# The last weight group of a two-layer encoder trunk, taken tile by tile

## The chip, the core and the metric

The kernel runs on one core of one Trainium2 chip. The metric is device time in microseconds (us), the median over runs of the whole program. One core has a matrix engine (TensorE, PE in the profile, with its weight loads as PEld), a vector engine (VectorE, DVE), a scalar engine (ScalarE, ACT), GpSimd (POOL) and SyncE (SP). SP and POOL issue DMA transfers here. The engines run their own instruction streams and wait for each other by semaphores.

## The reference

The program computes a two-layer encoder trunk for one sequence of 256 tokens with 2048 features, in float32. What matters for this change is the end:

```python
def rmsnorm(x, g):
    xf = x.astype(jnp.float32)
    y = xf * lax.rsqrt(jnp.mean(xf * xf, axis=-1, keepdims=True) + EPS)
    return (y * g.astype(jnp.float32)).astype(x.dtype)

def sq_relu_mlp(h, w1, w2):
    a = jax.nn.relu(h @ w1.astype(h.dtype))
    return (a * a) @ w2.astype(h.dtype)

    for layer in range(DEPTH):
...
        x = x + sq_relu_mlp(rmsnorm(x, f_norm[layer]), f_w1[layer], f_w2[layer])
    return rmsnorm(x, final_norm)
```

The hidden width of the MLP is 8192. The last operations are therefore the second MLP product of layer 1, its addition to x, and one more root-mean-square norm over the 2048 features of each token.

## The kernel before

**Layout.** Activations lie transposed: a feature is a partition, so x is 16 tiles of 128 features by 256 tokens, `x[:, t, :]`. All large weights come from one tensor `wts` in chunks of 1 MB (128 partitions by 2048 floats), in exactly the order in which they are used. 92 *groups* of four chunks each use them up; a group makes 512 output features (four tiles) from 2048 input features (16 tiles, `kt`). Groups 60 to 91 are the MLP of layer 1; it takes the hidden width in four quarters, each of four groups of the first product and four of the second. Group 91 is the last one and makes tiles 12 to 15 of x.

**Splitting.** Float32 precision comes from splitting each weight and each activation into a rounded part and a remainder of type fp32r, which PE multiplies faster than float32. ACT copies half a chunk (a *piece*, 128x1024) from `raw` to `whi` (L278), DVE subtracts it from `raw` into `wlo` (L579). `whi` and `wlo` have four slots each; a group is eight pieces, and PE frees a slot by counting up `half_free` after each piece. SP refills `raw` when `lo_ready` says that DVE is through with it (L242).

**A group on PE** (`group`, L1030 and L1032): for each piece, for each of its two `kt`, for each of four output tiles n, one product of `whi` with both parts of the activation (512 columns) into bank 4·par+n, and one of `wlo` with the rounded part (256 columns) onto the upper half of the same bank. So all four tiles of a group end together. `par` alternates between banks 0 to 3 and 4 to 7. The three operands are accumulated in two halves of a bank, which have to be added: ACT copies the upper halves into `cross` (L271, `copy_cross`), DVE adds the lower ones to it into `total` (L597, `leave_psum`), and adds that to x (L855, `onto_residual`).

**The norm.** Behind each group of the last quarter, `norm_part` has ACT square the four new tiles of x into `padded` (L316) and DVE sum them over the tiles (L619) into `ssum` (L625, L622). With the last of the four, PE multiplies `ssum` with a matrix of ones (L1065, `mean_squares`), which gives every partition the sum over all 2048 features; ACT takes the root (L323), DVE the reciprocal (L639, `rms_of`). Meanwhile ACT has multiplied x by the gain of the final norm into `conv`, one instruction per tile (L488). DVE multiplies four tiles at a time by `rms` (L985), and POOL sends each four tiles out, 512 KB, when they are ready (L262). One float32 product on PE, such as L1065, stands in the trace as two MATMUL records.

**Order.** Nothing is planned by a program: each engine's order is written out by hand. ACT and DVE split the weights of the *next* group between the steps of the present one (`split(G, 0)`, `split(G, 1)` and so on; piece k of it is piece k+3 of group G+1), so that during the steps of group 90 the last five pieces of group 91 are split, and nothing is left to split behind that. In the last quarter, PE runs the same loop as for the other ones; the loop body is 8 groups long.

## Time and profile before

| | us |
|---|---|
| median of 3 runs | 2287.17 |
| lowest and highest of these runs | 2283.44, 2287.83 |
| time of the profiled execution | 2285.45 |
| its span in the trace | 2283.5 |
| last record in the chain of waits, start | 2277.69 |
| output transfers, kind of queue and traffic | software_dynamic, 2.10 MB |
| granted clock over the span | 0.989 |

The page gives each engine's busy time as a share of the span; a chain followed back from the last instruction; groups of instructions by line, with the mean of one in ns. A *window* is the same for a stretch of time, and its clock column is the share of full speed (2.4 GHz) that TensorE was granted: 0.50 is the lower of its two levels, 1.2 GHz. DMA transfers have a time *to landing*, from issue to the end of their last packet. Between the last landing and the end of the span nothing stands in the trace.

### The profile page before, as it was taken

To read this page: it belongs to the slowest core of one execution; us is meant where nothing else is said; L and a number is where in the kernel's file an instruction comes from. 1 tells how busy PE (TensorE), PEld (TensorE's weight loads), DVE (VectorE), ACT (ScalarE), POOL (GpSimd) and SP (SyncE) were. 2 spreads that over 40 slices of the span, in tenths; PEclk is the share of its full clock that TensorE was granted. 3 is DMA by queue.
4 is the path that set the end of the run, shared out by engine and by line. 5 is a ranking of instruction groups with operands and counts; after the bars stand their busy time and mean duration, and the time that the engine had idled before them with its cause. 6 is when DMAs were issued, how large, how long until landed. Compare 5 with 4: busy or idle time off the path is not lost.

```text
span 2283.5 us, 36015 instructions
## 1 busy us (share of the span) xinstructions
PE 2198.2 (96%) x14110; PEld 2023.7 (89%) x14110; DVE 1562.1 (68%) x1809; ACT 972.6 (43%) x1042; POOL 11.5 (1%) x25
## 2 busy tenths in 40 slices
PE   7999999889999999999999999899999999999996
PEld 7988898889999999999999888788899999999995
DVE  8676567467765765765674999977665665665765
ACT  4544344344444544544442100155444444444553
POOL 0000000000000000000000000000000000000000
PEclk9999999999999999999999999999999999999998
DMA  6432233255555555555554444244555555555553
GB/s 226 178 112 91 98 123 121 84 193 185 202 204 202 198 193 211 197 198 197 203 201 148 151 158 153 76 163 167 203 199 198 192 206 200 201 202 202 199 192 123
DMA packets 55864, 396.84 MB, mean 174 GB/s; under 512 B 6497, under 2 KB 6881, under 8 KB 8545
## 3 DMA queue, kind: packets, MB, share of 16 engines
q1 hardware_dynamic: 54288, 389.32, 47.0%
q0 software_dynamic: 1488, 6.29, 1.0%
q8 instruction: 63, 1.03, 0.2%
q14 instruction: 25, 0.20, 0.0%
HBM read 393.49 MB, written 2.10 MB: 173 GB/s over the span
## 4 chain that ended last, share of the span: by engine, by line
PE 77%; DVE 14%; issue 4%; ACT 3%; DMA 2%; DVEq 0%; ACTq 0%; SPq 0%; POOL 0%
PE ps L1030 40%; PE ps L1032 20%; DVE work L925 4%; PE ps L1057 4%; DVE wlo L579 3%; PE ps L1005 3%; PE ps L1007 3%; PE ps L1009 3%; PE ps L1116 2%; DMA raw<-in_wts 1%; ACT whi L278 1%; DVE sq_part L619 1%; PE ps L1181 1%; PE ps L1180 1%; DVE work L686 0%
## 5 line engine op out<-in xcount | busy, mean ns | idle before, releaser
L579 DVE TENSOR_TENSOR wlo<-raw,whi 128x1024 fp32r<-128x1024 f32 x672 | 817.3, 1224 | 493.4 <-ACT whi L278 479.6
L278 ACT ACTIVATE whi<-raw 128x1024 fp32r<-128x1024 f32 x672 | 705.9, 1057 | 714.3 <-PE ps L1032 362.2
L1030 PE MATMUL ps<-hid,whi 128*128 128x512 f32 x2304 | 755.7, 382 | 5.8 <-DVE hid L958 3.3
L1030 PE MATMUL ps<-xg,whi 128*128 128x512 f32 x2048 | 672.0, 382 | 7.1 <-ACT sq_part L323 4.6
L1032 PE MATMUL ps<-hid,wlo 128*128 128x256 f32 x2304 | 628.0, 273 | 0.0
L1032 PE MATMUL ps<-xg,wlo 128*128 128x256 f32 x2048 | 558.2, 273 | 0.0
L1030 PEld LDWEIGHTS ps<-hid,whi 128*128 128x128 f32 x2304 | 435.4, 189 | 67.8 <-issue 3.9
L1032 PEld LDWEIGHTS ps<-hid,wlo 128*128 128x128 f32 x2304 | 442.4, 192 | 0.0
L1030 PEld LDWEIGHTS ps<-xg,whi 128*128 128x128 f32 x2048 | 387.1, 189 | 62.2 <-ACT sq_part L323 5.2
L1032 PEld LDWEIGHTS ps<-xg,wlo 128*128 128x128 f32 x2048 | 393.2, 192 | 0.0
L1005 PE MATMUL ps<-xg,whi 128*128 128x256 f32 x768 | 223.3, 291 | 11.1 <-DVE wlo L579 11.1
L1057 PE MATMUL ps<-work,raw 128*128 128x256 f32 x1024 | 221.5, 379 | 0.0
L1057 PEld LDWEIGHTS ps<-work,raw 128*128 128x128 f32 x1024 | 194.5, 190 | 26.4
L1007 PE MATMUL ps<-xg,whi 128*128 128x256 f32 x768 | 214.7, 280 | 0.0
L1009 PE MATMUL ps<-xg,wlo 128*128 128x256 f32 x768 | 214.3, 279 | 0.0
L925 DVE SCALAR_TENSOR_TENSOR work<-work,dwt 128x256 f32<-128x256 f32 (+1 forms) x492 | 195.5, 480 | 1.0 <-DVE work L908 0.9
L597 DVE TENSOR_TENSOR total<-ps,cross 128x1024 f32<-128x1024 f32 x68 | 98.8, 1453 | 100.3 <-ACT cross L271 97.2
L1005 PEld LDWEIGHTS ps<-xg,whi 128*128 128x128 f32 x768 | 150.8, 196 | 13.6 <-issue 12.7
L1007 PEld LDWEIGHTS ps<-xg,whi 128*128 128x128 f32 x768 | 151.0, 197 | 0.0
L1009 PEld LDWEIGHTS ps<-xg,wlo 128*128 128x128 f32 x768 | 150.9, 196 | 0.0
L271 ACT ACTIVATE cross<-ps 128x1024 f32<-128x1024 f32 x64 | 65.5, 1023 | 112.0 <-PE ps L1032 112.0
L505 ACT ACTIVATE total<-total,pt 128x256 f32<-128x256 f32 x16 | 7.3, 500 | 172.5 <-DVE total L902 172.5
(203 smaller groups left out, 1470.5 us busy)
## 6 DMA issues: line engine op xcount, KB each, us to landing
raw<-in_wts SPq DMA_DIRECT2D x368, 1024.0 KB, 4.8
x<-in_xt SPq DMA_DIRECT2D x4, 512.0 KB, 7.8
x<-in_xt POOLq DMA_DIRECT2D x1, 2048.0 KB, 9.7
out_t<-work POOLq DMA_DIRECT2D x4, 512.0 KB, 3.3
work<-in_rows POOLq DMA_DIRECT2D x12, 128.0 KB, 3.8
ct<-in_consts SPq DMA_DIRECT2D x1, 768.0 KB, 6.3
work<-in_w_s POOLq DMA_DIRECT2D x4, 128.0 KB, 4.3
dwt<-in_dw SPq DMA_DIRECT2D x1, 248.0 KB, 5.0
```

The costliest lines, as they stand in the source:

```text
L271: return nc.scalar.activation(dst, src, ACT.Copy)
L278: nc.scalar.activation(whi[:, i % SPLIT].rearrange("p a b -> p (a b)"), raw[:, r, HALF * (i % 2):HALF * (i % 2) + HALF], ACT.Copy).then_in ...
L579: tt(wlo[:, i % SPLIT].rearrange("p a b -> p (a b)"), raw[:, i // 2 % RAW, HALF * (i % 2):HALF * (i % 2) + HALF], whi[:, i % SPLIT].rearra ...
L597: tt(halves(total[:]), in_order(ps[:, 4 * par:4 * par + 4, 0:T]), in_order(cross[:]), ALU.add).then_inc(banks_free, 1)
L925: ins = stt(acc[t], src, w, acc[t], ALU.mult, ALU.add)
L1005: mm(dst, whi[:, r, k, cols], woven(operand[:, kt, 0, :]), start=(kt == 0 and n % 2 == 0), stop=False, skip_group_check=True)
L1007: mm(dst, whi[:, r, k, cols], woven(operand[:, kt, 1, :]), start=False, stop=False, skip_group_check=True)
L1009: ins = mm(dst, wlo[:, r, k, cols], woven(operand[:, kt, 0, :]), start=False, stop=(kt == KT - 1), skip_group_check=True)
L1030: mm(ps[:, 4 * par + n, :], whi[:, r, k, cols], woven_parts(operand[:, kt]), start=(kt == 0), stop=False)
L1032: ins = mm(ps[:, 4 * par + n, T:2 * T], wlo[:, r, k, cols], woven(operand[:, kt, 0, :]), start=False, stop=(kt == KT - 1))
L1057: ins = mm(ps[:, 4 * par + n, 0:T], raw[:, r, CH_N * k + P * n:CH_N * k + P * n + P], xf[:, kt, :], start=(kt == 0), stop=(kt == KT - 1))
L1116: ins = mm(bank(b)[:, h, :], left[:, h, :], right[:, h, :], start=True, stop=True)
```

## The change

Group 91 is done by a new function on PE, `last_group`, and by new tails on ACT and DVE.

- The weights of group 91 are laid out otherwise in `wts` (on the host, ahead of the run): a chunk is now one output tile with all 16 `kt`, instead of four `kt` of all four tiles. The number of bytes, chunks, pieces and splits is the same.
- PE takes tile after tile, two pieces each. Tiles 12 to 14 use the same two products as before, into banks 4 to 6. Tile 15 has three products of 256 columns instead, all into the lower half of bank 7, so that nothing is left to be added.
- ACT copies the upper half of one bank at a time, squares that tile of x once DVE has added it, and multiplies it by the gain. DVE adds and sums tile by tile (256 wide each). The sum of squares of tile 15 is not added by DVE: PE multiplies `padded[:, 3]` with the ones itself, onto the product of `ssum`, in bank 0.
- The last quarter of the layer-1 MLP is no longer part of PE's loop, but is written out behind it.
- The output leaves in five transfers (4, 4, 4, 2 and 2 tiles) that SP issues, no longer in four that POOL issues. DVE's last four tiles are multiplied in two instructions.

```diff
+OUT_TILES = [(0, 4), (4, 8), (8, 12), (12, 14), (14, 16)]
...
@@ sync
+            for n, (a, b) in enumerate(OUT_TILES):
+                sp.wait_ge(out_raw, n + 1)
+                sp.dma_start(out[:, a:b, :], conv[:, a:b, :]).then_inc(out_done, 16)
+            sp.wait_ge(out_done, 16 * len(OUT_TILES))
@@ gpsimd
-            for j in range(4):
-                pool.wait_ge(out_raw, j + 1)
-                pool.dma_start(out[:, CH_K * j:CH_K * j + CH_K, :], conv[:, CH_K * j:CH_K * j + CH_K, :]).then_inc(out_done, 16)
-            pool.wait_ge(out_done, 64)
@@ scalar
-                for j in range(4):
+                for j in range(3 if last_norm else 4):
                     G = base + 8 * q + 4 + j
...
-            root(4)
+            def gained(t):
+                return nc.scalar.activation(conv[:, t, :], x[:, t, :], ACT.Copy, scale=param("final_norm")[:, t:t + 1])
+
+            act.wait_ge(banks_free, G_END + 1)
+            act.wait_ge(ssum_part, 19)
+            for n in range(4):
+                if n < 3:
+                    act.wait_ge(half_free, SPLIT + 8 * (G_END - 1 - UNSPLIT) + 2 * n + 2)
+                    copy(cross[:, n, :], ps[:, 4 + n, T:2 * T]).then_inc(s["last_cross"], 1)
+                act.wait_ge(s["last_x"], n + 1)
+                nc.scalar.activation(padded[:, n, 0:T], x[:, 12 + n, :], ACT.Square).then_inc(s["last_sq"], 1)
+                ins = gained(12 + n)
+            ins.then_inc(s["gained"], 1)
+            root(4, at=0)
@@ vector
+            for n in range(4):
+                w = x[:, 12 + n:13 + n, :]
+                sums = in_order(ps[:, 4 + n:5 + n, 0:T])
+                if n < 3:
+                    dve.wait_ge(s["last_cross"], n + 1)
+                    link(tt(halves(total[:, n:n + 1, :]), sums, in_order(cross[:, n:n + 1, :]), ALU.add))
+                    tt(w, w, total[:, n:n + 1, :], ALU.add).then_inc(s["last_x"], 1)
+                    dve.wait_ge(s["last_sq"], n + 1)
+                    ins = tt(ssum[:], ssum[:], padded[:, n, 0:T], ALU.add)
+                    if n < 2:
+                        link(ins)
+                    else:
+                        ins.then_inc(ssum_ready, 1)
+                else:
+                    dve.wait_ge(half_free, SPLIT + 8 * (G_END - UNSPLIT))
+                    tt(halves(w), halves(w), sums, ALU.add).then_inc(s["last_x"], 1)
             rms_of(4)
-            for j in range(4):
-                dve.wait_ge(s["gained"], j + 1)
-                w = conv[:, 4 * j:4 * j + 4, :]
-                tt(w, w, by_token(rms[:], 4), ALU.mult).then_inc(out_raw, 1)
+            for a, b in OUT_TILES:
+                dve.wait_ge(s["gained"], min(a // 4 + 1, 4))
+                w = conv[:, a:b, :]
+                tt(w, w, by_token(rms[:], b - a), ALU.mult).then_inc(out_raw, 1)
@@ tensor
+            def last_group(G):
+                pe.wait_ge(banks_free, G + 1)
+                for i in range(8):
+                    pe.wait_ge(lo_ready, 8 * (G - UNSPLIT) + i + 1)
+                    n, r = i // 2, i % SPLIT
+                    hi, lo = (w[:, r].rearrange("p a (b c) -> p (a b) c", c=P) for w in (whi, wlo))
+                    for k in range(8):
+                        kt = 8 * (i % 2) + k
+                        first, last = kt == 0, kt == KT - 1
+                        if n < 3:
+                            mm(ps[:, 4 + n, :], hi[:, k, :], woven_parts(hid[:, kt]), start=first, stop=False)
+                            ins = mm(ps[:, 4 + n, T:2 * T], lo[:, k, :], woven(hid[:, kt, 0, :]), start=False, stop=last)
+                        else:
+                            mm(ps[:, 7, 0:T], hi[:, k, :], woven(hid[:, kt, 0, :]), start=first, stop=False)
+                            mm(ps[:, 7, 0:T], hi[:, k, :], woven(hid[:, kt, 1, :]), start=False, stop=False)
+                            ins = mm(ps[:, 7, 0:T], lo[:, k, :], woven(hid[:, kt, 0, :]), start=False, stop=last)
+                    ins.then_inc(half_free, 1)
+                pe.wait_ge(banks_free, G + 2)
+                pe.wait_ge(ssum_ready, 5)
+                mm(ps[:, 0, 0:T], const("ones"), ssum[:], start=True, stop=False)
+                pe.wait_ge(s["last_sq"], 4)
+                mm(ps[:, 0, 0:T], const("ones"), padded[:, 3, 0:T], start=False, stop=True).then_inc(ms_ready, 1)
...
-                with pe.Fori(1, NQ) as q:
+                with pe.Fori(1, NQ - layer) as q:
...
-            mean_squares(4)
+            base = G_MLP1 + 8 * (NQ - 1)
+            with pe.Fori(0, 2) as i:
+                for par in range(2):
+                    group(base + 2 * i + par, par, xg, None, 0, UNSPLIT)
+            for j in range(3):
+                group(base + 4 + j, j % 2, hid, hid_ready, 20 + 4 * (NQ - 1) + 1, UNSPLIT)
+            last_group(G_END - 1)
@@ kernel
+    w = a["f_w2"][1][(NQ - 1) * D:, D - CH_N:]
+    parts[-1][-4:] = w.reshape(KT, P, 4, P).transpose(2, 1, 0, 3).reshape(4, P, CH)
```

On DVE, the program's end before, from the last subtraction of a piece of group 91 to the last product with `rms`:

```order
L579 TENSOR_TENSOR wlo<-raw,whi 128x1024 [waits hi_ready]
L597 TENSOR_TENSOR total<-ps,cross 128x1024 [waits cross_ready]
L855 TENSOR_TENSOR x<-x,total 128x1024 [waits banks_free]
L619 TENSOR_REDUCE sq_part<-padded 128x256 [waits sq_ready,x_new]
L622 TENSOR_TENSOR ssum<-ssum,sq_part 128x256 [waits ssum_part]
L639 RECIPROCAL rms<-sq_part 128x256 [waits root_ready,ssum_ready]
L985 TENSOR_TENSOR work<-work,rms 128x1024 [waits gained,rms_ready]
L985 TENSOR_TENSOR work<-work,rms 128x1024 [waits gained] x3
```

The same place on DVE now (`work` is the memory of `conv`; `ps` is PSUM; three rows for each of the tiles 12 to 14, then the one that adds tile 15):

```order
L593 TENSOR_TENSOR wlo<-raw,whi 128x1024 [waits hi_ready]
L1000 TENSOR_TENSOR total<-ps,cross 128x256 [waits last_cross]
L1001 TENSOR_TENSOR x<-x,total 128x256 [waits dve_step]
L1003 TENSOR_TENSOR ssum<-ssum,padded 128x256 [waits last_sq]
L1000 TENSOR_TENSOR total<-ps,cross 128x256 [waits last_cross,dve_step]
L1001 TENSOR_TENSOR x<-x,total 128x256 [waits dve_step]
L1003 TENSOR_TENSOR ssum<-ssum,padded 128x256 [waits last_sq]
L1000 TENSOR_TENSOR total<-ps,cross 128x256 [waits last_cross,dve_step]
L1001 TENSOR_TENSOR x<-x,total 128x256 [waits dve_step]
L1003 TENSOR_TENSOR ssum<-ssum,padded 128x256 [waits last_sq]
L1010 TENSOR_TENSOR x<-x,ps 128x256 [waits half_free]
L653 RECIPROCAL rms<-sq_part 128x256 [waits root_ready]
```

The reduction over four tiles is gone; nine instructions stand in its and the addition's place ahead of the one that waits for the last product (L1010).

On ACT, the end of the program before, behind the last copies of pieces:

```order
L278 ACTIVATE whi<-raw 128x1024 [waits half_free,raw_in1] x2
L271 ACTIVATE cross<-ps 128x1024 [waits banks_free,half_free]
L316 ACTIVATE padded<-x 128x4x256 [waits ssum_part,x_new]
L488 ACTIVATE work<-x,pt 128x256 x4
L323 ACTIVATE sq_part<-ps,pt 128x256 [waits ms_ready]
```

And the same place on ACT now:

```order
L278 ACTIVATE whi<-raw 128x1024 [waits half_free,raw_in1] x2
L271 ACTIVATE cross<-ps 128x256 [waits half_free,ssum_part,banks_free]
L571 ACTIVATE padded<-x 128x256 [waits last_x]
L562 ACTIVATE work<-x,pt 128x256
L271 ACTIVATE cross<-ps 128x256 [waits half_free]
L571 ACTIVATE padded<-x 128x256 [waits last_x]
L562 ACTIVATE work<-x,pt 128x256
L271 ACTIVATE cross<-ps 128x256 [waits half_free]
L571 ACTIVATE padded<-x 128x256 [waits last_x]
L562 ACTIVATE work<-x,pt 128x256
L571 ACTIVATE padded<-x 128x256 [waits last_x]
L562 ACTIVATE work<-x,pt 128x256
```

The copy of a tile's upper half now stands behind the square and the gain of the tile before, and L323 (the root) follows as before.

## Rows read from the trace of the kernel before

**Rows 1.** Page, part 1: busy time of each engine.

```profile
PE 2198.2 (96%) x14110; PEld 2023.7 (89%) x14110; DVE 1562.1 (68%) x1809; ACT 972.6 (43%) x1042; POOL 11.5 (1%) x25
```

**Rows 2.** Windows; columns: stretch, its length, busy PE, PEld, DVE, ACT, POOL, clock, DMA.

```profile
2263.50:2284.00 20.50, 1.22 (x2) 0.50 (x2) 10.72 (x9) 3.12 (x6) 2.14 (x4) 0.55 0.25 102
```

**Rows 3.** Chain that ended last, from 2262: start, length, what.

```profile
2262.00 1.03 ACT cross L271
2263.06 1.24 DVE total L597
2264.32 1.24 DVE x L855
2265.58 1.06 ACT padded L316
2266.73 1.91 DVE sq_part L619
2268.67 0.43 DVE ssum L622
2269.15 1.24 PE ps L1065 x2
2270.41 0.48 ACT sq_part L323
2270.98 1.76 DVE rms L639
2272.77 1.22 DVE work L985
...
2275.13 2.28 DVE work L985 x2
...
2277.69 0.53 POOL out_t L262
```

**Rows 4.** Groups by form, whole run: drain of four tiles, one-tile copy from PSUM.

```profile
L597 DVE TENSOR_TENSOR total<-ps,cross 128x1024 f32<-128x1024 f32 x68 | 98.8, 1453 | 100.3 <-ACT cross L271 97.2 <-ACT cross L305 2.5 <-DVE rms L639 0.5
L305 ACT ACTIVATE cross<-ps,pt 128x256 f32<-128x256 f32 x16 | 6.2, 471 | 1.5 <-PE ps L1032 1.5
```

**Rows 5.** Timeline of PE, products of an early group, then of the last: start, length.

```profile
199.84 0.28 PE L1005 MATMUL ps<-xg,whi 128*128 128x256 f32 x1
...
202.18 0.28 PE L1005 MATMUL ps<-xg,whi 128*128 128x256 f32 x1
...
2254.92 0.38 PE L1030 MATMUL ps<-hid,whi 128*128 128x512 f32 x1
...
2261.47 0.38 PE L1030 MATMUL ps<-hid,whi 128*128 128x512 f32 x1
```

**Rows 6.** Timeline of DVE and ACT while the last group runs.

```profile
2253.30 2.36 DVE L579 TENSOR_TENSOR wlo<-raw,whi 128x1024 fp32r<-128x1024 f32 x2
...
2246.95 1.69 ACT L488 ACTIVATE work<-x,pt 128x256 f32<-128x256 f32 x4
```

**Rows 7.** Windows as rows 2, straight PE code and behind it; then timeline of PE.

```profile
1612.00:1696.00 84.00, 84.00 (x513) 77.22 (x514) 59.87 (x49) 41.45 (x40) 0.00 (x0) 1.00 0.54 194
2262.00:2266.00 4.00, 0.00 (x0) 0.00 (x0) 2.45 (x2) 1.45 (x2) 0.00 (x0) 0.93 0.00 0
...
1600.54 0.60 PE L1065 MATMUL ps<-ssum,ct 128*128 128x256 f32 x2
```

**Rows 8.** Output transfers: landing; DMA rate in 40 slices of 2270 to 2283.5.

```profile
DMA to landing us min/median/max: 2.9/3.3/3.6
...
GB/s 0 0 0 0 0 0 0 0 0 0 0 0 0 0 0 0 449 413 425 267 388 388 400 376 352 400 413 376 376 400 425 352 12 0 0 0 0 0 0 0
```

**Rows 9.** Page, part 6, landing on SP; then DMA rate, 40 slices of 0.5:12.

```profile
raw<-in_wts SPq DMA_DIRECT2D x368, 1024.0 KB, 4.8
pt<-in_params SPq DMA_DIRECT2D x1, 97.5 KB, 2.1
...
GB/s 0 0 0 0 52 228 310 299 399 228 256 413 342 413 399 456 427 370 342 399 427 342 399 413 456 485 442 456 456 370 456 427 399 399 342 413 413 442 413 427
```

More of the change, by code:

```diff
@@ L159, in build @@
             "glu_scaled", "gate", "taps0", "taps1", "pivot_sum", "pivot", "acc_init", "first_ln_d", "ln_sq", "ln_stats",
-            "ln_var", "ln_root", "ln_norm", "ln_act", "gained")}
+            "ln_var", "ln_root", "ln_norm", "ln_act", "gained", "last_cross", "last_x", "last_sq")}
         block = ctx.enter_context(nc.Block())
@@ L319, in norm_part, with root @@
                     copy(xg[:, 4 * j:4 * j + 4, 0, :], total[:]).then_inc(xg_hi, 1)
-            def root(n):
+            def root(n, at=7):
                 act.wait_ge(ms_ready, n + 1)
-                nc.scalar.activation(sq_part[:], ps[:, 7, 0:T], ACT.Sqrt, scale=1.0 / D, bias=eps).then_inc(root_ready, 1)
+                nc.scalar.activation(sq_part[:], ps[:, at, 0:T], ACT.Sqrt, scale=1.0 / D, bias=eps).then_inc(root_ready, 1)
             eps, eps_q = param("eps"), param("eps_q")
@@ L882, in mlp @@
                     split(G, 3, 4, 5, 6, 7, skipped=skipped)
-                for j in range(4):
+                for j in range(3 if last and layer else 4):
                     G = base + 8 * q + 4 + j
@@ L980, in _ @@
             mlp(G_MLP1, 1, NQ - 1, True, None)
+            for n in range(4):
[14 more added lines that the diff above has]
+                    tt(halves(w), halves(w), sums, ALU.add).then_inc(s["last_x"], 1)
             rms_of(4)
-            for j in range(4):
-                dve.wait_ge(s["gained"], j + 1)
-                w = conv[:, 4 * j:4 * j + 4, :]
-                tt(w, w, by_token(rms[:], 4), ALU.mult).then_inc(out_raw, 1)
+            for a, b in OUT_TILES:
+                dve.wait_ge(s["gained"], min(a // 4 + 1, 4))
+                w = conv[:, a:b, :]
+                tt(w, w, by_token(rms[:], b - a), ALU.mult).then_inc(out_raw, 1)
         @block.tensor
```

## The prediction

> **What bounds the kernel now.** I start with the busy shares. PE is busy for 96% of the span and no other engine for more than 68% [rows 1]; up to its last product the kernel is as fast as PE gets through its matmuls. This change takes no matmul away, so no gain can come from there, and the next view is the window in which PE is not busy. From 2263.5 to the end, 20.5 us, PE works for 1.22 us [rows 2]. The tail behind the last product is thus a chain of single steps, and the chain of waits gives it in order [rows 3]: the last product ends at 2262.0 (ACT starts at 2262.00), then ACT copy, DVE add, DVE add to x, ACT square, DVE reduction, DVE sum, PE product, ACT root (begins at 2270.41), DVE reciprocal, and from 2272.77 the four multiplications with rms, 1.14 us apart (2.28 for two). The last transfer is issued at 2277.69. From 2262.0 to 2283.5 that is 21.5 us: 8.41 us until the root begins, 2.36 from there to the first multiplication, and 10.7 for multiplying and sending. The reader is to see that nearly every step of the first stretch handles four tiles (1024 wide), although each is independent of the other tiles, and that PE stands idle meanwhile.
>
> **Part 1: the products of group 91.** Tiles 12 to 14 have the same products in another order. A pair (512 and 256 columns) is issued every (2261.47 - 2254.92) / 20 = 0.3275 us, 20 pairs lying between the two rows shown [rows 5]. Tile 15 has 48 products of 256 columns in place of 16 pairs. In the early groups, which use that form, 21 products lie between the two rows shown, (202.18 - 199.84) / 21 = 0.1114 us each [rows 5]. So tile 15 takes 48 x 0.1114 = 5.35 us, not 16 x 0.3275 = 5.24: +0.11. Those early products also go into one bank three at a time, which is the nearest row for what is new in tiles 12 to 14, several products in a row into the same bank. The weights' pieces come in the same number and order, and DVE has the last one ready at 2253.30 + 2.36 = 2255.66 [rows 6], while PE needs it at about 2262.1 - 2.7 = 2259.4. The last quarter's products are now straight code: from 1612 to 1696 PE runs such code and is busy for 84.00 of 84.00 us [rows 7]. I cost it at nothing; fetching instructions is hidden by the products before.
>
> **Part 2: does the tile chain keep up?** DVE is free at 2255.66, when tiles 12 and 13 (ends of their products: 2262.0 less 15.7 and 10.5 us) are done and tile 14 (2256.8) nearly is, so DVE and ACT set the pace, not PE. No row shows these 256-wide forms, except DVE's sum over SBUF, 0.43 us [rows 3], and ACT's copy from PSUM, 0.47 [rows 4]. Reading PSUM while PE writes there costs DVE 1.453 us for four tiles (mean of 68), and 1.24 where PE is idle [rows 4, 3]; I take 0.43 x 1.453 / 1.24 = 0.50 for L1000. ACT instructions in a row follow every 1.69 / 4 = 0.42 us [rows 6]. Each handoff costs about 0.04 (from 2262.00 + 1.03 to 2263.06, for instance) [rows 3]. One round: DVE add 0.54, DVE onto x 0.46, ACT square 0.51, ACT gain 0.42, ACT copy of the next tile 0.42, sum 2.35 us. DVE's order is strict: its sum for tile 14 stands ahead of L1010. It ends at 2255.69 + 2 x 2.35 + (0.50 + 0.46 + 0.51 + 0.04 + 0.43) = 2262.33. Tile 15's products end at 2261.98 + 0.11 = 2262.09. So L1010 starts at 2262.36, 0.27 us late. That is the only queueing in front of it; PE's product with ssum waits for the same sum, runs 2262.4 to 2263.0, and is hidden by the two steps that follow.
>
> **Part 3: what is left behind the last product.** From 2262.36: DVE onto x 0.45 (PE idle, so close to 0.43), ends 2262.81; ACT square 0.04 + 0.47, ends 2263.32; PE 0.05 + one product. That product took 1.24 us before [rows 3] and 0.60 where PE had just worked (at 1600.54) [rows 7]. The granted clock explains the ratio: in the first four microseconds without work it was 0.93 on average [rows 7], by 2263.5 and later 0.55 on average [rows 2], half of full speed being the lower level of 1.2 GHz. PE now pauses for about 0.4 us twice, so I take 0.60; 1.24 is the other end. It ends at 2263.97. Root and reciprocal keep their 0.03 + 2.36 us, so the multiplications begin at 2266.36 instead of 2272.77: **-6.41 us**. Of that, the four wide steps (copy, two additions, square, with gaps 4.73) become two narrow ones (0.96), the reduction and the sum (2.42) go, the product shrinks by 0.64, and 0.38 comes back from parts 1 and 2. The gain for tile 15 stands on ACT behind its square, 0.42 us, beside PE's 0.60. It is hidden; without that cover it would cost 0.42.
>
> **Part 4: the output.** Before, counted from the first multiplication M = 2272.77: last issue M + 4.92, landing 3.3 later [rows 8], M + 8.2. Data flowed in slices 17 to 32 of that window, from 2275.4 to 2280.9, 2.10 MB in 5.5 us [rows 8]. Now three multiplications at 1.14 and two of half that width (estimate 0.62 each, between 0.43 and 1.14 less a little) end at M + 4.7. SP issues at once, where POOL was 0.30 late at its last (2277.69 against 2277.41) [rows 3]. A landing on SP took 2.1 us for 97.5 KB and 4.8 for 1024 KB [rows 9], by which 256 KB takes 2.1 + 158.5 / 926.5 x 2.7 = 2.6: M + 7.3. The other bound is flow: SP's first issue at M + 1.26, data 1.1 us later as at POOL, and 5.5 us for the 2.10 MB, M + 7.8. On SP's queue, transfers at the program's start flowed at about 400 GB/s [rows 9], no slower than these. The later of the two decides, 7.8 against 8.2; I take **-0.5**, ends +1.3 (a last landing of 4.8 us) and -0.9. The remaining 2.5 us between landing and end I leave as they are.
>
> On this handoff the Trainium skill, DMA: Bandwidth & Descriptors, section Latency and other measured facts, gives SP's hardware queue about 0.6 us to the first byte and GpSimd's about 1. The trace shows 1.1 on POOL and nothing as clean on SP under load. By that rule the sum would be some 0.4 us lower, 2279.9; I leave it out.
>
> **Sum.** 6.4 + 0.5 = 6.9 us. Against the profiled execution: span 2283.5 becomes 2276.6, time 2285.45 becomes 2278.5. That execution lay 1.7 us below the median of 2287.17, so for a median I say **2280.2 us**. A difference under 0.2% (4.6 us) cannot be told from none here; the three runs shown lie 4.4 us apart.
>
> **Rivals.**
> 1. *The tile chain lags.* If each narrow instruction costs nearer to one of half a group than to a quarter (0.69 for 512 wide as an estimate from 1.24 and 0.43), a round is 3.4 us and tile 14's sum ends at about 2255.7 + 2 x 3.4 + 2.9 = 2265.4, 3.1 us later than worked out; the steps of part 3 grow by 0.5. The gain is 3.3 us, 2283.9. For it: every step depends on another engine, and rounds have no slack. Against: 0.43 and 0.47 are measured for this width.
> 2. *The end behind the last landing is POOL's.* 2.5 us pass there, from 2280.9 to 2283.5 [rows 8]. If they are POOL's way of noticing the end, SP may save up to 2: 2278.2. For: nothing in the trace fills the gap. Against: any queue must report its writes. The skill, same page, section Anatomy of one DMA, puts most of a fixed 2 us down to the confirmation that the last byte has landed, heaviest for HBM; by this rule the gap stays. No run here shows which.
> 3. *The output gets slower on SP*: small transfers on one queue, the last one with the landing of a large one, 4.8 us: M + 9.5, so +1.3 instead of -0.5. Gain 5.1, 2282.1. Against: SP's rate at the start.
> 4. *Slower.* Successive products into one bank wait for each other. If a pair takes 0.38 + 0.27 us, the durations of its records, in place of 0.3275, 48 pairs cost 48 x 0.32 = +15.5 and the kernel takes 2295.7. It decides from 6.9 / 48 = 0.14 us per pair. Against: the early groups put three products in a row into one bank at 0.1114 each [rows 5], with records of 0.28. What differs is only that the second product covers half of the first one's columns.
> 5. *PE's clock falls all the same*, or its short pauses cost a slow product: +0.64, 2280.8; this lies inside the forecast's range.
>
> **Chances.** Forecast, with 5 as its edge, 0.64 (2278.5 to 2282); rival 1, 0.10; rival 2, 0.14; rival 3, 0.08; rival 4, 0.04. Faster by over 0.2% holds in the forecast and rival 2 nearly always, and in most of rival 3: 0.82. Rival 1 and what run-to-run noise takes from the others give no difference: 0.14. Slower: 0.04. The range has to hold rivals 1 to 3 and a median's noise of about 2 us: 2276 to 2284.5; it leaves out rival 4 and the edges of 1 and 2.
>
> **What would show it.** In the profile after: PE busy without gap until about 2262.1, products of group 91 in pairs every 0.33 us and at last every 0.11; the instruction before L1010 on DVE ending near 2262.3, and DVE waiting neither long for ACT nor the reverse; the last product with the ones at 0.60, not 1.24, and a granted clock near 1 there; the reciprocal beginning near 2264.5; the last landing 7.3 to 7.8 us after the first multiplication. Idle PE inside group 91, or pairs above 0.33, would be rival 4; a sum of tile 14 that ends after 2263 would be rival 1; a gap under 2 us behind the last landing, rival 2.

## The result and the profile after

The changed kernel takes 2271.89 us in the median of 4 runs (2270.95 to 2273.26), against 2285.31 for the kernel before, measured beside it (4 runs, 2283.01 to 2287.83). The ratio is 0.9948 with a 95% interval of 0.9935 to 0.9961: faster, by 9 to 15 us, where I had forecast 2280.2 and a gain of 6.9. The direction was right. The time lies below my range of 2276 to 2284.5. Of all timed runs named below, one, of the kernel called unrolled, took 8122.76 us; it is left out of that kernel's median.

The profiled execution has a span of 2269.2 us, 14.3 less than before. The chain of waits of the changed kernel, from the last three products on (start, length, what), answers to [rows 3]:

```profile
2256.80 0.11 PE ps L1081
2256.91 0.11 PE ps L1082
2257.02 0.13 PE ps L1083
2257.14 0.02 issue
2257.17 0.43 DVE x L1010
2257.60 0.02 issue
2257.62 0.42 ACT padded L571
2258.05 0.04 issue
2258.09 0.71 PE ps L1089 x2
2258.80 0.02 issue
2258.83 0.48 ACT sq_part L323
2259.31 0.02 issue
2259.34 1.76 DVE rms L653
2261.10 0.02 issue
2261.12 1.23 DVE work L1015
```

Three things are to be read in it. The step from the last product to the first multiplication, M, took 10.79 us before (2261.98 to 2272.77) and takes 3.97 now: 6.82 gained, where I had 6.41 with the lateness of parts 1 and 2 taken off. From M to the end of the span it was 10.73 us and is 2269.2 - 2261.12 = 8.08: 2.65 gained, where I had 0.5. And the last product itself ends at 2257.15 instead of 2261.98, 4.83 us earlier, where I had 0.11 later. 6.82 + 2.65 + 4.83 = 14.3.

The output on the queue of SP: its five issues on the timeline, the landing, and the DMA rate in 40 slices from 2262 to 2269.2 (answers to [rows 8]):

```profile
2262.37 4.01 SPq L246 DMA_DIRECT2D out_t<-work  x5
...
DMA to landing us min/median/max: 2.6/2.9/3.0
...
GB/s 0 0 0 0 0 0 159 387 455 387 410 410 478 387 433 432 387 387 501 410 387 455 387 410 410 478 410 296 432 410 387 399 410 432 307 23 0 0 0 0
```

The fifth transfer is issued at 2265.85 and lands 2.9 us later, at 2268.8, that is 0.4 us before the end. Before, the last issue at 2277.69 landed 3.6 us later, at 2281.3, and 2.2 us followed. The packets end before that: at 2280.9 before, and here in the slice that begins at 2268.3. The landing is thus not the end of the last packet, as I wrote ahead of the prediction, but lies 0.4 us behind it in both kernels; SP's own wait for the output ends at 2268.8 too.

The drain that ran beside the products, in groups by form from 2250 to 2258.5, with what ended the idle time ahead of each, shows that DVE was in time, where part 2 had expected it late:

```profile
L1000 DVE TENSOR_TENSOR total<-ps,cross 128x256 f32<-128x256 f32 x3 | 1.3, 445 | 0.6 <-ACT cross L271 0.6
L1003 DVE TENSOR_TENSOR ssum<-ssum,padded 128x256 f32<-128x256 f32 x3 | 1.3, 426 | 1.4 <-ACT padded L571 1.4
...
L1010 DVE TENSOR_TENSOR x<-x,ps 128x256 f32<-128x256 f32 x1 | 0.4, 420 | 0.3 <-PE ps L1083 0.3
```

L1010 waits 0.3 us for PE's last product; the product does not have to wait for DVE. A round took 2.12 us (L1001 at 2251.28, 2253.40 and 2255.53).

### The profile page after: what moved, and what is told of

Same layout as the page of the kernel before. It is cut to its first block, busy times and chain, and to the rows that moved or that the text cites. A ratio compares the mean times of both kernels' runs of the same rounds, so it can differ in the third digit from the quotient of the medians.

```text
span 2269.2 us, 36017 instructions
## 1 busy us (share of the span) xinstructions
PE 2192.6 (97%) x14128; PEld 2018.7 (89%) x14128; DVE 1561.8 (69%) x1816; ACT 972.7 (43%) x1047; POOL 9.4 (0%) x21
## 4 chain that ended last, share of the span: by engine, by line
PE 77%; DVE 14%; issue 4%; ACT 3%; DMA 2%; DVEq 0%; ACTq 0%; SPq 0%
PE ps L1060 39%; PE ps L1062 20%; DVE work L939 4%; PE ps L1112 4%; DVE wlo L593 3%; PE ps L1035 3%; PE ps L1039 3%; PE ps L1037 3%; PE ps L1171 2%; DMA raw<-in_wts 1%; ACT whi L278 1%; DVE sq_part L633 1%; PE ps L1235 1%; PE ps L1236 1%; DVE work L700 0%
## 5 line engine op out<-in xcount | busy, mean ns | idle before, releaser
L1060 PE MATMUL ps<-hid,whi 128*128 128x512 f32 x2240 | 734.8, 382 | 5.6 <-DVE hid L972 3.3
L1062 PE MATMUL ps<-hid,wlo 128*128 128x256 f32 x2240 | 610.6, 273 | 0.0
L1060 PEld LDWEIGHTS ps<-hid,whi 128*128 128x128 f32 x2240 | 423.3, 189 | 66.0 <-issue 3.9
L1062 PEld LDWEIGHTS ps<-hid,wlo 128*128 128x128 f32 x2240 | 430.1, 192 | 0.0
L271 ACT ACTIVATE cross<-ps 128x1024 f32<-128x1024 f32 (+1 forms) x66 | 65.7, 996 | 103.1 <-PE ps L1062 102.7
```

Of the source, the lines that this page charges most:

```text
L271: return nc.scalar.activation(dst, src, ACT.Copy)
L1060: mm(ps[:, 4 * par + n, :], whi[:, r, k, cols], woven_parts(operand[:, kt]), start=(kt == 0), stop=False)
L1062: ins = mm(ps[:, 4 * par + n, T:2 * T], wlo[:, r, k, cols], woven(operand[:, kt, 0, :]), start=False, stop=(kt == KT - 1))
```

## Where the 4.8 us ahead of the last product come from

Nothing in the change touches the program ahead of group 84, yet the second root of the layers (root 2) came at 1248.32 before and at 1243.81 after. Windows in the mixer stage show where. First the kernel before, then the changed one (columns as in rows 2; the clock is the third number from the right):

```profile
184.00:188.00 4.00, 3.86 (x19) 2.33 (x20) 0.73 (x1) 0.09 (x1) 0.00 (x0) 0.84 0.46 164
188.00:192.00 4.00, 4.00 (x20) 3.78 (x19) 1.68 (x4) 2.18 (x3) 0.00 (x0) 0.50 0.23 98
...
412.00:416.00 4.00, 1.61 (x12) 1.42 (x11) 1.83 (x2) 1.19 (x2) 0.00 (x0) 0.93 0.00 0
416.00:420.00 4.00, 4.00 (x26) 4.00 (x25) 0.69 (x1) 0.60 (x1) 0.00 (x0) 0.65 0.02 4
```

```profile
184.00:188.00 4.00, 4.00 (x25) 2.51 (x26) 0.51 (x2) 0.03 (x1) 0.00 (x0) 1.00 0.52 174
188.00:192.00 4.00, 3.64 (x31) 3.45 (x32) 3.00 (x5) 3.10 (x4) 0.00 (x0) 1.00 0.21 88
...
412.00:416.00 4.00, 3.83 (x34) 3.83 (x35) 0.81 (x2) 0.93 (x2) 0.00 (x0) 1.00 0.02 4
```

Before, TensorE ran at 1.2 GHz (0.50) from 186.7 to 193.6 and from 415.4 to 418.8 us, behind pauses of PE of 0.9 and 2.4 us and small products; after, with the same instructions and the same pauses there, it stayed at 2.4 GHz. From 188 to 192 PE handled 20 products before and handles 31 now.

The question for the experiments was thus double: is the clock's better luck a work of the change, and what shortened the output? Theory A: the clock's drops are drawn anew by every run. Rival B: the change prevents them.

## Experiments

All kernels of a comparison ran on the same chip beside runs of the kernel before. The table gives what their profiles show: P, the end of the last product of group 91; the path from there to the first multiplication, M; and from M to the end of the span. All in us.

| kernel | P | P to M | M to end | span | median (runs) |
|---|---|---|---|---|---|
| before | 2261.98 | 10.79 | 10.73 | 2283.5 | 2285.7 (74) |
| changed | 2257.15 | 3.97 | 8.08 | 2269.2 | 2271.89 (4) |
| again | 2258.05 | 3.98 | 8.07 | 2270.1 | 2271.21 (5) |
| again2 | 2263.99 | 3.97 | 8.04 | 2276.0 | 2277.04 (6) |
| again3 | 2258.73 | 3.99 | 8.08 | 2270.8 | 2274.89 (6) |
| out_sp4 | 2255.85 | 10.79 | 7.96 | 2274.6 | 2282.95 (11) |
| tail_pool4 | 2263.75 | 3.97 | 10.68 | 2278.4 | 2278.19 (7) |
| unrolled | 2257.15 | 10.79 | 10.66 | 2278.6 | 2285.85 (11) |
| sp_waits | 2256.25 | 10.78 | 9.67 | 2276.7 | one run |
| pool_waits | 2258.44 | 10.79 | 9.47 | 2278.7 | one run |

**The same kernel again (again, again2, again3).** No edit.

> The changed kernel once more, unaltered. Theory A (the part of the gain ahead of the last group, 4.8 us between the two profiled executions, is how TensorE's clock happened to be granted in the mixer stage, and varies from run to run with either kernel): the median gain over the kernel before lies between 9.4 and 13 us, and some runs of before come within 10 us of some runs of this one. Rival B (the change itself makes the early part faster): the gain is 13 to 14.5 us in every round, and the profile again has its mixer stage 4 to 5 us shorter than before's.

> The changed kernel a third time, unaltered. So far its nine runs lay between 2269.6 and 2274.3, while the kernel that differs from it only in the sizes of the output transfers had three of six runs between 2275.2 and 2278.1. Theory A1 (the clock's state in the mixer stage is drawn by each run alike for either kernel; the first nine runs were lucky): some of these runs lie above 2275, and over all its runs the kernel's median is 2272 to 2275. Theory A2 (this program always starts in the spared state): none above 2274.5.

> The changed kernel a fourth time. Theory (its advantage is 9.45 us at an equal state of the clock, and both kernels draw that state alike): over all its runs the mean comes to 2274 to 2276, 9.5 to 11 us below before's 2285.1. Rival B (something of the change also spares the clock's drops): the mean stays at 2273 or below.

Measured: ratios to before 0.994 (0.9927 to 0.9953), 0.9967 (0.9955 to 0.9979) and 0.9954 (0.9941 to 0.9967). The first gain is 14.8 us between the medians, more than theory A allowed, so again seemed to favour rival B. Again2 did not: five of its six runs lie above 2275, and its profile has the drops of the clock:

```profile
184.00:188.00 4.00, 3.47 (x17) 1.74 (x17) 1.12 (x1) 0.47 (x1) 0.00 (x0) 0.82 0.38 113
188.00:192.00 4.00, 4.00 (x18) 3.78 (x18) 1.31 (x2) 1.89 (x3) 0.00 (x0) 0.50 0.35 150
...
412.00:416.00 4.00, 1.62 (x12) 1.43 (x11) 1.83 (x2) 1.41 (x2) 0.00 (x0) 0.91 0.00 0
```

Its P is 2263.99, later than before's, and its two tail terms are 3.97 and 8.04 all the same. Over all 21 runs of the changed kernel the mean is 2273.9 (2269.6 to 2280.7), over 74 runs of before 2285.1 (2279.3 to 2290.0): 11.2 us, with 1.4 either way for a 95% interval taken from the scatter of both. That is above theory A's 9.5. The mean of 2273.9 lies just outside both forecasts of again3 (2274 to 2276 for theory A, 2273 or less for rival B), so the means alone don't decide.

The profiles do. In all 14 of kernels without added products, the two drops come both or not at all, and whether they come goes with a moment long before anything that the change touches: where, at 42 to 45 us, the clock falls for the first time.

| first fall of the clock | profiles | drops at 184 and 412 | root 2 |
|---|---|---|---|
| 42.0 to 42.2 | changed, unrolled, one_root | no | 1243.7 to 1244.0 |
| 42.7 to 43.4 | before, again2, tail_pool4, sum_on_dve | yes | 1247.6 to 1248.7 |
| 44.1 to 44.7 | again, again3, out_sp4, sp_waits, pool_waits, tile15_pairs, out_early | no | 1242.5 to 1243.2 |

A fall at 43.2 and one at 44.2 look like this (again2, then again3):

```profile
40.00:44.00 4.00, 1.26 (x10) 1.07 (x9) 3.90 (x5) 3.36 (x4) 0.00 (x0) 0.90 0.51 213
...
40.00:44.00 4.00, 1.92 (x16) 1.68 (x15) 3.93 (x5) 2.95 (x4) 0.00 (x0) 1.00 0.46 184
```

Either kind of kernel stands in the rows with drops and without: four of the five with before's code up to P were spared, and six of the nine with the changed tail. That is theory A: the drops are a matter of the run, and rival B, that the change prevents them, is out.

**PE's last quarter written out, alone (unrolled).**

```diff
-                with pe.Fori(1, NQ) as q:
+                with pe.Fori(1, NQ - layer) as q:
...
             mlp(G_MLP1, 1)
+            base = G_MLP1 + 8 * (NQ - 1)
...
+            for j in range(4):
+                group(base + 4 + j, j % 2, hid, hid_ready, 20 + 4 * (NQ - 1) + 1, UNSPLIT)
             mean_squares(4)
```

> The kernel before with only PE's last quarter of the layer-1 MLP written out behind its loop; nothing else is changed, so the tail is the same and no product is added or taken away. Theory A: the tail takes 21.5 us as before and the median is within 2.5 us of before's. Rival B in the form that the code's layout sets the pace of the early part: 4 to 5 us faster, mixer stage shorter, tail the same. Rival C (straight code costs fetch stalls): idle TensorE inside groups 84 to 91, slower by a microsecond or more.

Measured: ratio 1.0003 (0.9993 to 1.0013), tail 21.45. Its one profile has no drops at 184 and 412 and P at 2257.15, as the changed kernel, and yet its median is before's. So the straight code neither gains nor costs anything clear of the noise, and the early P is no sign of the change.

**The two drops of the clock, taken away from the kernel before (before_fill2) and from the changed one (after_fill2).** Products of the matrix of ones with a constant, which nobody reads:

```diff
+                        if (b, lev) == (3, 3):
+                            fill(5, 4)
                         pe.wait_ge(s["z"], LEVELS * b + lev)
...
+                        if (b, cc) == (0, 0):
+                            fill(2, 7)
                         pe.wait_ge(s["v_copy"], 2 * b + cc + 1)
...
                         ins.then_inc(s["s_prod"], 1)
+                        if (b, cc) == (0, 0):
+                            fill(2, 7)
```

> The kernel before with nine products whose result nobody reads, on PE alone: four around the first chunk of block 0 of the mixer (at about 183 to 188 us) and five while PE waits for the third level of block 3 (about 412 us). These are the two places where the profile of before shows TensorE's clock at half and that of the changed kernel does not. Tail as before. Theory A (the 4.8 us ahead of group 91 are these two drops of the clock, which come in some runs and not in others): the granted clock stays at 1.00 at 184 to 196 and 412 to 420 us, root 2 comes at 1243 to 1245 us instead of 1248.3, the median is 3 to 5 us below before's, near 2282, and the runs lie closer together than before's 10 us. Rival D (the drops follow from something else that is late there, and cost nothing by themselves): clock up, median within 1 us of before's, or above by the 1 to 2 us that the products take.

> The changed kernel with the same nine products. Theory A with the guess that the changed kernel is nearly always spared the two drops: no gain, 0 to 1.5 us slower than the changed kernel (2271.2), that is 2271 to 2273. Against before_fill2 it is then 9.5 us faster, the sum of the tail's two parts (6.8 and 2.65), which is what the change is worth apart from the clock. Rival B (the change makes the early part faster in another way): more than 12 us faster than before_fill2.

Measured: before_fill2's clock stays up at both places:

```profile
188.00:192.00 4.00, 4.00 (x34) 3.72 (x32) 1.71 (x4) 2.64 (x4) 0.00 (x0) 1.00 0.54 225
...
416.00:420.00 4.00, 3.16 (x28) 2.97 (x27) 1.94 (x3) 1.08 (x2) 0.00 (x0) 1.00 0.00 0
```

Root 2 comes at 1245.30, 3.0 us earlier than before's. That the clock stays up is the work of the products and not of a lucky run: the first falls of both kernels are at 43.3 and 42.8 us, the row of the table in which the drops come. The median is 2283.78 against 2285.29 (ratio 0.9992, 0.9983 to 1.0000), 1.5 us, half of the least that I expected. The nine products cost something themselves: root 2 is at 1245.3 and 1245.1, 1 to 3 us later than in the profiles without fillers that were spared. But the 11 runs of before_fill2 lie within 3.3 us (2282.4 to 2285.7), the 23 runs of before beside it within 9.2. So the scatter of this kernel is for the most part these two drops. The changed kernel's did not narrow so far: the five runs of after_fill2 lie within 4.5 us. Its median is 2275.95, 7.8 below before_fill2, above what I expected of it (2271 to 2273) and far from rival B's 12 us. Its profile lost more to drops at places that I had not filled, at 1493 and 1609 us: from root 2 to P it took 1018.2 us, before_fill2 (with one short drop, at 1610) 1015.4, the changed kernel's first profile (with none) 1013.3.

**SP as the output's queue, alone (out_sp4), and the tail alone (tail_pool4).**

```diff
+OUT_TILES = [(0, 4), (4, 8), (8, 12), (12, 16)]
...
+            for n, (a, b) in enumerate(OUT_TILES):
+                sp.wait_ge(out_raw, n + 1)
+                sp.dma_start(out[:, a:b, :], conv[:, a:b, :]).then_inc(out_done, 16)
+            sp.wait_ge(out_done, 16 * len(OUT_TILES))
...
-            for j in range(4):
-                pool.wait_ge(out_raw, j + 1)
...
-            pool.wait_ge(out_done, 64)
```

> The kernel before with one part of the change: SP issues the output, in four transfers of 512 KB as before; the last group and its tail are as before. Theory (the queue of SP lands sooner and the 2.2 us between landing and end belong to POOL's queue): from the first multiplication with rms to the end of the span 8.3 to 8.8 us instead of 10.7, so 2 to 2.5 us are gained. Rival (the size of the last transfers does it, 256 KB instead of 512): 10 us or more remain, and under 0.8 us is gained. For the part ahead of group 91 theory A expects a shift of either sign, of up to 5 us; rival B, if the queue is the cause of it, expects -4 to -5.

> The changed kernel with the output as before: POOL issues it in four transfers of 512 KB, and DVE multiplies four times four tiles. The tile-by-tile tail stays. Theory: last product to first multiplication 4.0 us as in the changed kernel (10.8 before), first multiplication to end 10.5 to 10.8 as before, so 6.8 us are gained in the tail, plus whatever the early part does (theory A: anything from -5 to +3; rival B: -4 to -5 again, unless the output's queue was the cause). Rival for the tail: the 2.65 us of the output hang on something else than the queue and stay here.

Measured: out_sp4 keeps 10.79 and has 7.96 from M to the end, so the queue, issue and wait together, gives 2.77 and the sizes of the last transfers nothing (0.9988, 0.9977 to 0.9999). Tail_pool4 has 3.97 and 10.68 (0.9966, 0.9956 to 0.9977). The two terms are independent, and both profiles agree with the changed kernel's and before's to 0.12 us. (The spans are read to 0.1 us, so that these last digits are good to about 0.05.)

**Who issues and who waits (sp_waits, pool_waits).** In sp_waits `pool.wait_ge(out_done, 64)` of the kernel before goes to SP; in pool_waits the last wait of out_sp4 goes to POOL.

> The kernel before, in which POOL still issues the four output transfers, but SP instead of POOL waits for them to be done. Theory W (the 2.2 us behind the last landing are POOL's, which notices the semaphore late): 0.4 to 0.5 us behind the last landing, first multiplication to end about 8.9 us instead of 10.73. Theory Q (they belong to transfers whose descriptors POOL makes, whoever waits): 10.7 us as before.

> The kernel before, in which SP issues the four output transfers (as in out_sp4), but POOL waits for them to be done. Theory W: the 2.2 us behind the last landing are back, first multiplication to end 9.7 us instead of out_sp4's 7.96. Theory Q: 7.9 to 8.1 us.

Measured, from M to the end:

| | POOL waits | SP waits |
|---|---|---|
| POOL issues | 10.73 (before) | 9.67 (sp_waits) |
| SP issues | 9.47 (pool_waits) | 7.96 (out_sp4) |

Both theories hold by half. The waiting engine is worth 1.06 to 1.51 us, the issuing one 1.26 to 1.71. The last landing is 3.6 us behind its issue where POOL issues and 2.9 where SP does, whoever waits. Behind it the span goes on for 2.2 us (before), 1.1 (sp_waits), 1.9 (pool_waits) and 0.4 (out_sp4). So who waits acts only behind the landing. Who issues acts ahead of it, with 0.25 us (POOL issues 0.28 after the multiplication, SP 0.03) and 0.7 for the landing, and by the remaining 0.3 to 0.7 behind it too. Each of these times comes from one profile, but 2.2 and 0.4 came again, to 0.1 us, in every profile with the same two engines. What the waiting engine does in them no profile shows.

**Another cut of the output (out_early)**: `OUT_TILES = [(0, 2), (2, 6), (6, 10), (10, 14), (14, 16)]`.

> The changed kernel with the output in five transfers of 2, 4, 4, 4 and 2 tiles instead of 4, 4, 4, 2 and 2: the first is issued about 0.57 us earlier. Theory (the flow of 2.10 MB at some 400 GB/s bounds the output, the first issue decides): first multiplication to end 7.5 to 7.7 us instead of 8.07. Rival (the last issue and its landing of 2.9 us bound it): 8.0 to 8.2, no gain. In the median 0.5 us is below what can be told.

Measured: M to end 8.00, against 8.08 no more than the reading's error, so the rival was right. The last issue and its landing bound the output, not the flow.

**Two parts of the tail undone (tile15_pairs, sum_on_dve) and one step more (one_root).** The first uses the two products and `cross` for tile 15 too; the second is

```diff
-                mm(ps[:, 0, 0:T], const("ones"), ssum[:], start=True, stop=False)
-                pe.wait_ge(s["last_sq"], 4)
-                mm(ps[:, 0, 0:T], const("ones"), padded[:, 3, 0:T], start=False, stop=True).then_inc(ms_ready, 1)
+                mm(ps[:, 0, 0:T], const("ones"), ssum[:], start=True, stop=True).then_inc(ms_ready, 1)
...
+                    dve.wait_ge(s["last_sq"], 4)
+                    tt(ssum[:], ssum[:], padded[:, 3, 0:T], ALU.add).then_inc(ssum_ready, 1)
```

and the third

```diff
-            root(4, at=0)
+            act.wait_ge(ms_ready, 5)
+            nc.scalar.activation(rms[:], ps[:, 0, 0:T], ACT.Abs_reciprocal_sqrt, scale=1.0 / D, bias=eps).then_inc(root_ready, 1)
+            gained(15).then_inc(s["gained"], 1)
...
-            rms_of(4)
+            dve.wait_ge(root_ready, 5)
```

> The changed kernel with tile 15 done like the three before it: two products per input tile into both halves of bank 7, then ACT's copy and DVE's addition of the halves. Theory (a narrow copy and a narrow addition come back on the path, 0.02 + 0.38 and 0.05 + 0.45, and 48 products of 0.1114 us become 16 pairs of 0.3275): last product to first multiplication 4.8 to 4.9 us instead of 3.97, tail 0.8 us longer in all. Rival (the three products into one half of a bank cost more than they spare): M is earlier, not later.

> The changed kernel with DVE adding the squares of tile 15 to ssum and one product with the ones behind it, instead of a second product onto the first. Theory: 0.04 + 0.43 us come on the path; last product to first multiplication 4.4 to 4.5 us instead of 3.97, with PE's last product near 0.70 as now, since PE idles for only 1.4 us before it and the clock stays. Rival (the pause lets the clock fall): that product takes 1.2 us and the path 4.9 to 5.0.

> The changed kernel with the root (ACT) and the reciprocal (DVE, 1.75 us) replaced by one ACT instruction that makes the reciprocal root, and with ACT's gain of tile 15 moved behind it; its results are not bit for bit those of the other two. Theory: the reciprocal goes, but ACT loads another table, 1.28 us, from the end of the last square on; it ends about 0.5 us after PE's product, so the path becomes 0.90 (onto x, square) + 1.28 + 0.03 + 0.48 + 0.03 = 2.75 us from last product to first multiplication instead of 3.97: 1.2 us gained. Rival (the table is loaded only when the product is there): 1.65 + 1.28 + 0.5 = 3.5 us, 0.5 gained.

Measured: in tile15_pairs P to M is 4.86, 0.89 more, as worked out. In sum_on_dve it is 0.53 more from the addition for tile 15 to M (2263.55 to 2268.03), with PE's last product at 0.68: the clock stayed, the rival is out. One_root has 2.71 instead of 3.97. Its chain shows the table load (L575, 1.28) beginning right behind the square, as the theory had it (the 0.49 behind it is the reciprocal root itself):

```profile
2259.48 0.43 DVE x L1012
2259.91 0.02 issue
2259.94 0.42 ACT padded L571
2260.35 0.02 issue
2260.37 1.28 ACT L575
2261.65 0.49 ACTq L66
2262.15 0.02 issue
2262.17 1.23 DVE work L1017
```

The medians of the three (2273.80, 2275.54, 2274.98) can't be ranked by such steps: the clock moves them more.

**Filling more waits (after_fill5, root_fill4).** After_fill5 fills, beside the two places, the waits at 119 and before 1449 us, and puts 14 products ahead of PE's wait for `o_norm` of block 3. Root_fill4 is one_root with the two places, the wait at 119 and 12 products ahead of the wait for `gv_norm` of group 11.

> The changed kernel with the nine products and 34 more of the kind: seven while PE waits at about 119 us, 14 at about 473 us, 13 at about 1446 us, the three waits after which the clock was at half in every profile so far. Theory A carried further: the clock stays at 1.00 behind each of them. Behind 119 and 473 PE has weights' products to do at half speed, 3.4 and 6.8 us long, each costing up to half of its length, 1.7 and 3.4 us; behind 1449 it is 6.8 us, partly waiting. The median is 2265 to 2268. Rival: PE does not bound these stretches (VectorE does), the clock is up and the median is 2270 to 2273.

> The kernel one_root with products that nobody reads in four waits of PE: nine at 183 to 188 and 412 us as in before_fill2, seven in the wait at 119 us, and 12 in the wait of 6.6 us at 471 us, where this time the wait is PE's own (the product with the mixer's second weights). Theory: the clock stays at 1.00 behind 122, 184, 412 and 476 us; where it stood at half for 6.8 us after 476, 48 and more products at 0.21 us become 0.11, 3 us gained, and about 1 us behind 122; the median is 2267 to 2270 and the runs lie within 5 us. Rival (the products delay what comes behind them as they did in after_fill5): 2274 or more.

Measured: after_fill5 had a mean clock of 0.995 in its profile and was 7 us slower than the changed kernel (means 2281.1 and 2273.9; its median 2281.48; ratio to before 0.9987, 0.9978 to 0.9995). Both theory and rival failed: the clock fell all the same at 482 and 1451 us, and at 212, where it had stayed up in the changed kernel's first profile. The 14 products stood on PE at 450.0 for 6.2 us at a wait that is not the one PE idles in, and what followed came 5.8 us later; the 13 of the last place made DVE wait 2.5 us. That was my reading of the code, not of the clock. Root_fill4, with the right wait, has the lowest median of all: 2270.40 of 5 runs (2268.8 to 2273.2), ratio 0.9935 (0.9922 to 0.9948), just above what I expected. 1.26 of that is one_root's shorter path. It has no drop at the four places:

```profile
120.00:128.00 8.00, 6.78 (x43) 5.59 (x42) 7.92 (x12) 4.33 (x7) 0.00 (x0) 1.00 0.36 131
184.00:192.00 8.00, 7.59 (x54) 5.71 (x53) 3.51 (x6) 3.42 (x5) 0.00 (x0) 1.00 0.37 131
412.00:420.00 8.00, 6.94 (x56) 6.32 (x55) 3.49 (x5) 1.66 (x2) 0.00 (x0) 1.00 0.04 5
476.00:484.00 8.00, 4.84 (x35) 4.17 (x34) 6.80 (x10) 1.83 (x3) 0.00 (x0) 1.00 0.50 188
```

At 476 the clock is up but PE is busy for no longer than in the changed kernel (5.13 there, at 0.61), and DVE, busy for 6.80 of these 8 us, seems to bound the stretch. The 3 us expected there did not come. Drops at 214, 1449 and 1606 us are left.

## Why the prediction was wrong

By its own steps:

- **Part 1, products: right.** In group 91 of the changed kernel 48 pairs lie between 2235.89 and 2251.28 (first to last), 0.3274 us each, and the 48 products of tile 15 follow each other every 0.11 us, as in the early groups. From root 3 (at 1611.41 and 1606.46) to P it takes 650.57 us before and 650.69 after, 0.12 more. Rival 4, the bank that waits, did not come.
- **Part 2, the drain: right in kind, too careful in size.** 2.12 a round instead of 2.35, because ACT's square of one tile takes 0.42, not the 0.47 that I took from L305, its copy 0.36 instead of 0.42, and DVE's addition from PSUM 0.445 instead of 0.50. The lateness of 0.27 vanished. Rival 1 did not come.
- **Part 3, the path: right.** Steps 0.43, 0.42, 0.71 and root with reciprocal 2.29; I had 0.45, 0.47, 0.60 and 2.36. The window of 2257 to 2259 has a clock of 1.00, so PE's 0.71 is not the lower clock. Five profiles agree on 0.70 for this product, behind a pause of 0.4 to 0.5 us, and have 0.60 or 0.67 for L1087, directly behind other products; whether the pause makes the difference is not shown. tile15_pairs and sum_on_dve show the two shortcuts to be worth 0.89 and 0.5 of the 6.82.
- **Part 4, the output: the step that failed.** "The remaining 2.5 us between landing and end I leave as they are", and rival 2, which had them shrink, had 0.14. They did not stay. Before, the gap was 2.2 us and the last landing 3.6 (I had put the median landing, 3.3, on the last transfer); now they are 0.4 and 2.9. With a last issue 0.2 us earlier that is the 2.65 us gained, 2.15 more than I gave. The experiments split it between the engine that waits for the output and the one that issues it. The flow of 5.5 us, which I let decide, was no bound: out_early moved it and gained 0.08. SP's first data came 0.7 to 0.9 us behind the first issue, where I had 1.1. The Trainium skill, DMA: Bandwidth & Descriptors, section Anatomy of one DMA, lays most of the fixed cost of a transfer to the confirmation of its last byte. Such a confirmation lies ahead of the landing, and from the last packet to the landing it is 0.4 us in both kernels. The gap that I was looking at lies behind the landing, and 1.06 to 1.51 us of it went with the waiting engine alone (10.73 to 9.67, 9.47 to 7.96).
- **The base.** I subtracted from 2287.17, a median of three. Over 74 runs before's mean is 2285.1: 2.1 us of the miss.
- **What I had no term for: TensorE's clock.** I read that it fell at the end, and not that it fell in the mixer stage, where the page's part 2 shows a busy PE. The 4.83 us between the two profiles are for the most part its drops at 184 and 412 us: 4.5 of them are there at root 2. They are not the change's: the kernels with before's code up to P have P at 2262.0, 2255.9, 2257.2, 2256.3 and 2258.4, the changed kernel in its four profiles at 2257.2, 2258.1, 2264.0 and 2258.7. The first four timed runs, with a mean of 2272.0, were 1.9 us luckier than the mean of all 21.

The sum of the miss, 2280.2 - 2272.0 (mean of the four) = 8.2, within rounding: tail 9.47 instead of 6.9, 2.6; base 2.1; luck of these runs 1.9; the rest, 1.7, is the difference between the 11.2 us of the means and the 9.47 of the profiles. It lies just outside the interval of 1.4. 0.2 of it is time outside the span: a run takes 2.0 us more than its span in the kernel before and 1.8 in the changed one. For the other 1.5 no profile shows a place, since P is not earlier in the changed kernel on average. The clocks on record point to the draws of the clock once more: their mean is 0.9918 over the 21 runs of the changed kernel and 0.9889 over 70 of before, so that 6.6 us more of full clock are missing before. Its longer tail, most of it at the lower clock, makes 4.9 of them. The 1.7 us that are left are an estimate, uncertain by as much, so this part stays open.

The Trainium skill, TensorE: Matmul & The Clock Gate, Part 1, says that the gate's timing does not begin anew with a kernel, so that the same kernel shows different numbers of slow matmuls from run to run. The runs here agree: 44.2 us against 43.2 for the first drop in again3 and again2, the same kernel, and drops at 184 and 412 in the second and not in the first. The page puts the penalty of the slow start under 1% of a typical span and would not model it; here the two drops in mid-kernel made 0.2%, half of the effect to be predicted.

## What to carry to other kernels

Behind the last product every step is latency: take the drain tile by tile while the matrix engine still works, leave one narrow tile for the end, and price it from rows of that width; this came out to 0.4 us. Have the output both issued and waited for by SyncE, which was worth 2.8 us here: the stretch behind the last landing is a term to be priced like any other. Before believing a difference of some 5 us, compare a landmark that the change cannot reach, such as the end of the last product here; where it moved, take the clock by windows, and more than one profile. A median of three or four runs can be 2 us off.

## What the runs showed of the hardware

- Waiting for the last transfers on POOL instead of SP made the span 1.06 and 1.51 us longer, with the same transfers. All of it lies behind the last landing. The last landing itself took 3.6 us from POOL and 2.9 from SP.
- TensorE's granted clock fell to 1.2 GHz at two places of the mixer stage in some executions and stayed at 2.4 in others, with the same instructions; ahead of the one at 415 us PE had paused for 2.4 us, in either case. In 14 profiles the two drops came when the first fall of the clock was at 42.7 to 43.4 us, and not when it was at 42.0 to 42.2 or 44.1 to 44.7. With them root 2 came 3.6 to 6.3 us later.
- Nine unread products at these places kept the clock up and narrowed the scatter of the kernel before from 9.2 us (23 runs) to 3.3 (11 runs), at a gain of 1.5 us in the median.
- The two matmul records of a float32 product behind a pause of 0.4 to 0.5 us took 0.70 us at full clock, directly behind other products 0.60 or 0.67; at the lower clock it took 1.24.
- The table load of ACT (1.28 us) began 0.02 us behind the square, ahead of the product that its instruction waits for (one_root).
